# First expert weights loaded during routing, unused expert rows filled during the chunk scan, expert blocks run in pairs from block 0

## The reference, cut to what matters

```python
n_assign = n_tok * TOP_K
counts = jnp.bincount(flat_e, length=N_EXPERTS)
pcounts = (counts + (MOE_BLOCK - 1)) // MOE_BLOCK * MOE_BLOCK     # MOE_BLOCK = 128
pends = jnp.cumsum(pcounts); pstarts = pends - pcounts
dest = pstarts[se] + (arange(n_assign) - starts[se])
...
hdn = silu(xb @ w1[e]) * (xb @ w3[e])                            # w1, w3: 1024 x 512
return hdn @ w2[e]                                               # w2: 512 x 1024
...
y_assign = ybuf[dest] * sw[:, None]
y = segment_sum(y_assign, stok)
```

## Time and profile before

| | |
|---|---|
| time, median of 3 runs | 3274.21 us (3272.35 to 3277.04) |
| span of the profiled execution | 3280.3 us |
| the chunk scan's first load starts | 926.36 us |
| routing's last instruction starts (`idx`) | 2082.98 us |
| first expert matmul starts | 2101.44 us |
| last expert matmul starts | 3161.42 us |
| `combine` starts | 3165.65 us |
| PE busy, whole span | 2858.0 us (87%) |

### The profile page before, as it was taken

One profiled execution on the slowest core, in us unless ns is written; L12 is line 12 of the kernel. 1 busy time (PEld: TensorE's weight loads), 2 busy tenths in 40 slices (PEclk: granted clock), 3 DMA queues, 4 the chain that ended last, 5 costly groups with the idle time before them and its releaser, 6 DMA issues. The chain is left out here.

```text
span 3280.3 us, 48264 instructions
## 1 busy us (share of the span) xinstructions
PE 2858.0 (87%) x16338; PEld 2528.5 (77%) x16339; DVE 2044.5 (62%) x2266; ACT 974.9 (30%) x1814; POOL 1239.3 (38%) x929
## 2 busy tenths in 40 slices
PE   5999999999879999999997997497899999999940
PEld 4998989989758888888886886376777788778730
DVE  5464564645446766666673333879768567877836
ACT  5152341524422222222222221122223222223223
POOL 3010111001056666556662221443445445434434
PEclk6999999999989999999998998699999999999975
DMA  4011111111111110111104442489476566767649
GB/s 148 32 56 36 52 61 37 55 35 54 33 42 39 38 32 26 38 38 38 39 20 137 153 138 93 155 300 348 174 261 260 214 249 238 270 221 273 246 151 342
DMA packets 223030, 424.40 MB, mean 129 GB/s; under 512 B 14465, under 2 KB 103649, under 8 KB 222818
## 3 DMA queue, kind: packets, MB, share of 16 engines
q1 hardware_dynamic: 201984, 340.35, 29.7%
q0 software_dynamic: 13328, 55.06, 4.6%
q10 hardware_dynamic: 7634, 27.79, 2.1%
HBM read 343.31 MB, written 87.18 MB: 131 GB/s over the span
## 5 line engine op out<-in xcount | busy, mean ns | idle before, releaser
L450 PE MATMUL project_proj<-hT_high,project_w_high 128*128 128x412 f32 (+3 forms) x1392 | 496.5, 357 | 28.5 <-issue 10.9
L450 PE MATMUL project_proj<-hT_low,project_w_high 128*128 128x412 f32 (+3 forms) x1392 | 474.8, 341 | 0.0
L450 PE MATMUL project_proj<-hT_high,project_w_low 128*128 128x412 f32 (+3 forms) x1392 | 474.8, 341 | 0.0
L817 POOL TENSOR_TENSOR delta_M<-delta_lt,lvl 128x512 f32<-128x512 f32 x252 | 331.9, 1358 | 58.5 <-DVE delta_lt L1031 58.5
L1584 DVE TENSOR_TENSOR experts_w_low<-experts_w_whole,experts_w_high 128x2048 fp32r<-128x2048 f32 x128 | 349.3, 2729 | 4.4
L1678 PE MATMUL experts_h<-experts_w_high,experts_xT_high 128*128 x848 | 338.0, 399 | 12.0 <-POOL experts_xT_low L1628 7.8
L1678 PE MATMUL experts_h<-experts_w_low,experts_xT_high 128*128 x848 | 337.6, 398 | 0.0
L1678 PE MATMUL experts_h<-experts_w_high,experts_xT_low 128*128 x848 | 336.0, 396 | 0.0
L450 PEld LDWEIGHTS project_proj<-hT_high,project_w_high 128*128 128x128 f32 (+1 forms) x1392 | 261.3, 188 | 45.6 <-issue 31.9
L1582 DVE CAST experts_w_high<-experts_w_whole 128x2048 fp32r<-128x2048 f32 x128 | 190.8, 1491 | 169.2 <-DMA experts_w_whole<-in_w_dram 169.1
L866 PE MATMUL delta_prep<-delta_Tm,delta_M 128*128 128x128 f32 x1728 | 245.0, 288 | 49.8 <-DVE delta_qkT L1045 40.0
(11 more groups left out here) (270 smaller groups left out, 5727.5 us busy)
## 6 DMA issues: line engine op xcount, KB each, us to landing
experts_w_whole<-in_w_dram SPq DMA_DIRECT2D x128, 1024.0 KB, 10.5
experts_w_whole<-in_w_dram SPq DMA_DIRECT2D x32, 2048.0 KB, 18.4
delta_qkv<-feat SPq DMA_DIRECT2D x36, 768.0 KB, 4.7
y_rows<-experts_yout ACTq DMA_DIRECT2D x53, 512.0 KB
project_w_whole<-in_w_tiles_dram SPq DMA_DIRECT2D x28, 512.0 KB, 3.7
feat<-project_out SPq DMA_DIRECT2D x48, 205.0 KB, 1.9
normalise_x<-in_x_dram SPq DMA_DIRECT2D x18, 512.0 KB, 3.3
output_xres<-in_x_dram SPq DMA_DIRECT2D x18, 512.0 KB, 5.7
```

What stands on the lines that cost most here:

```text
L450: r = pe.matmul(dst, w[s][:, kt, 0:m], x[:, kt, lo:hi], start=kt == 0 and i == 0, stop=kt == KD - 1 and i == 2)
L817: pool.tensor_tensor(v["M"][:, l], v["lt"][:, :, :], bcast(k["lvl"][:, d, l, :], HEADS, 1), ALU.mult).then_inc(e["M_set"], 1)
```

## The change

Four things are done, all around the experts.

- `MAXB`, the largest number of blocks, is rounded to an even number (68, was 67), and the loop over pairs begins with the blocks 0 and 1. With 52 blocks, 52 run instead of 53. The last block to run, an odd number, comes from a new entry of `table`, which DVE writes at the end of routing.
- `empty_rows` is gone from POOL's loop. Instead SP fills, at the head of the chunk scan, all rows of `y_rows` from block `MINB` = 36 on: two DMAs of 2048 rows (8 MB each) from the input `x` to `y_rows`, ahead of the first load of the scan. Experts' blocks overwrite what is theirs later.
- A class `Weights` owns the weight buffers and is built ahead of `route`. SP loads w1, w3 and w2 of expert 0 and w1 and w3 of expert 1 while routing runs, and `experts` begins with expert 2 on SP. The wait for the first gather, which stood between two parts of expert 0's loads, goes with them.
- `ones`, `lower` and `lg` are placed at the other end of SBUF, and two index tiles become one; no instruction of theirs changes.

```diff
-MAXB += 1 - MAXB % 2
+MAXB += MAXB % 2
+MINB = 2 * T // P
...
+            rest = SLOTS - MINB * P
+            for half in range(2):
+                sp.dma_start(y_rows[MINB * P + half * rest // 2:MINB * P + (half + 1) * rest // 2, :], dram["x"][0:rest // 2, :]).then_inc(filled, 16)
             run(sp, step)
+            sp.wait_ge(filled, 32)
...
+        @block.sync
+        def _(sp):
+
+            weights.load_w13(sp, dram, 0, 0)
+            weights.load_w2(sp, dram, 0, 0)
+            weights.load_w13(sp, dram, 1, 1)
...
+            link(dve.tensor_scalar(tf[:, NE:NE + 1], end[:, NE - 1:NE], 1.0, None, ALU.subtract))
+            link(dve.tensor_copy(table[:, 2 * MAXB + NE + 1:2 * MAXB + NE + 2], tf[:, NE:NE + 1]))
+            link(dve.tensor_single_scalar(table[:, 2 * MAXB + NE + 1:2 * MAXB + NE + 2], table[:, 2 * MAXB + NE + 1:2 * MAXB + NE + 2], 1, ALU.bitwise_or))
             dve.wait_ge(placed, 1)
...
             step(0, 0, 0)
-            with eng.Fori(0, PAIRS) as j:
-                with eng.If(j * 2 + 1 < n):
+            step(1, 1, 0)
+            with eng.Fori(1, PAIRS) as j:
+                with eng.If(j * 2 < n):
+                    step(0, j * 2, j)
                     step(1, j * 2 + 1, j)
-                    step(0, j * 2 + 2, j + 1)
-                if and_then is not None:
-                    and_then(j)
+
+        def last_block(eng):
+            return eng.value_load(table[0:1, NB + 1:NB + 2], min_val=1, max_val=MAXB - 1)
...
-            load_w13(0, 0, PARTS[0:2])
-            sp.wait_ge(gathered, 16)
-            load_w13(0, 0, PARTS[2:])
-            load_w13(1, 1)
-            load_w2(0, 0)
...
-            def empty_rows(j):
...
-                with pool.If(j * -2 + (2 * PAIRS - 1) >= n):
-                    dst = y_rows[bass.ds(j * (-2 * P) + (2 * PAIRS - 1) * P, 2 * P), :]
-                    pool.dma_start(dst, xn_rows[0:2 * P, :]).then_inc(emptied, 16)
-                    pool.wait_ge(emptied, j * 16 + 16)
...
-            last = n // 2 * 2
+            last = last_block(pe)
             turn_gated(last)
             output(last)
```

More of the change, by code:

```diff
@@ L756, in delta @@
         E = [{n: b.sem(f"{n}{d}") for n in sems} for d in range(2)]
+        filled = b.sem("rows_filled")
         block = ctx.enter_context(nc.Block())
@@ L1317, in _, with __init__, load_w13, load_w2 @@
                     split(p, j * 2 + p)
-def route(nc, k, lg, gate, slot, table, idx):
+PARTS = [(n, q) for n in ("w1", "w3") for q in range(2)]
+KQ = KD // 2
+class Weights:
+    def __init__(self, nc, b):
+        whole, lows = over(nc, b, ("w1", "w3"), [P, 2, KD, FF])
+        self.whole, self.low = dict(zip(("w1", "w3"), whole)), dict(zip(("w1", "w3"), lows))
+        (self.w2_whole,), (self.w2_low,) = over(nc, b, ("w2",), [P, 2, FF // P, D])
+        self.w_sem = [{n: b.sem(f"moe_{n[0]}_{n[1]}_{p}") for n in PARTS} for p in range(2)]
+        self.w2_sem = [b.sem(f"moe_w2_{p}") for p in range(2)]
+    def load_w13(self, sp, dram, p, x):
+        for n, q in PARTS:
+            sp.dma_start(self.whole[n][:, p, q * KQ:(q + 1) * KQ],
+                         dram[n][bass.ds(x, 1), q * KQ * P:(q + 1) * KQ * P, :].rearrange("a (k p) n -> p (a k) n", p=P)).then_inc(self.w_sem[p][n, q], 16)
+    def load_w2(self, sp, dram, p, x):
+        sp.dma_start(self.w2_whole[:, p], dram["w2"][bass.ds(x, 1)].rearrange("a (k p) n -> p (a k) n", p=P)).then_inc(self.w2_sem[p], 16)
+def route(nc, k, dram, weights, lg, gate, slot, table, idx):
     with ExitStack() as ctx:
@@ L1484, in _, with experts @@
             dve.tensor_copy(idx[:, :], marked[:, :])
-def experts(nc, k, dram, table, idx, xn_rows, y_rows):
+def experts(nc, k, dram, weights, table, idx, xn_rows, y_rows):
     with ExitStack() as ctx:
@@ L1496, in experts @@
         pair = lambda name, shape, dt=F32: [b.sb(f"{name}{p}", shape, dt) for p in range(2)]
-        whole, lows = over(nc, b, ("w1", "w3"), [P, 2, KD, FF])
-        W = {n: (b.sb(f"{n}_high", [P, 2, KD, FF], F32R), low, w) for n, low, w in zip(("w1", "w3"), lows, whole)}
+        W = {n: (b.sb(f"{n}_high", [P, 2, KD, FF], F32R), weights.low[n], weights.whole[n]) for n in ("w1", "w3")}
         raw, xl = over(nc, b, ("xT0", "xT1"), [P, KD, P])
-        (w2_whole,), (w2_low,) = over(nc, b, ("w2",), [P, 2, FF // P, D])
+        w2_whole, w2_low = weights.w2_whole, weights.w2_low
         w2_high = b.sb("w2_high", [P, FF // P, D], F32R)
-        ix, xg = pair("ix", [P, 1], I32), b.sb("xg", [P, D])
+        both_ix, xg = b.sb("ix", [P, 2], I32), b.sb("xg", [P, D])
+        ix = [both_ix[:, p:p + 1] for p in range(2)]
         xh = pair("xT_high", [P, KD, P], F32R)
@@ L1573, in _ @@
             sp.wait_ge(e["done"], end_of(NE - 3))
-            load_w2(1, NE - 1)
+            weights.load_w2(sp, dram, 1, NE - 1)
         @block.vector
@@ L1660, in _ @@
             low(0, 0)
-            through_blocks(pool, n, step, empty_rows)
-            gated_low(n // 2 * 2)
+            through_blocks(pool, n, step)
+            gated_low(last_block(pool))
         @block.tensor
@@ L1780, in _ @@
             through_blocks(act, n, step)
[L1781 to L1785, removed]
+            last = last_block(act)
+            turned_gate(last)
+            act.wait_ge(e["gated_set"], last + 1)
+            output(last)
+            act.wait_ge(y_free, last * 16 + 32)
             act.sem_inc(e["all_stored"], 1)
@@ L1937, in encoder @@
                 with nc.cleanup_on_exit():
-                    delta(nc, k, gates, feat, O)
+                    delta(nc, k, dram, gates, feat, O, y_rows)
                 with nc.cleanup_on_exit():
                     output(nc, k, dram, feat, O, lg, x2_rows, xn_rows)
-        route(nc, k, lg, gate, slot, table, idx)
+        weights = Weights(nc, b)
+        route(nc, k, dram, weights, lg, gate, slot, table, idx)
         until_routed.close()
-        experts(nc, k, dram, table, idx, xn_rows, y_rows)
+        experts(nc, k, dram, weights, table, idx, xn_rows, y_rows)
         combine(nc, k, dram, gate, slot, x2_rows, y_rows, y)
```

35 lines of the change are left out of this document (12 added, 23 removed).

## The result

The changed kernel takes 3297.04 us (median of 4 runs, 3291.15 to 3297.58), the kernel before beside it 3275.62 (4 runs): a ratio of 1.0063, 95% interval [1.0049, 1.0078], or 21 us slower. The prediction was 3291.9 (3279 to 3310), slower.

The account below looks back on a forecast made before the run. Phases run in sequence; the scan is a PE-busy chain that cannot catch up, the experts PE-bound with a DVE-bound stretch. 44.6 - 9.2 - 17.7 = +17.7 us on a median of 3274.2 gives 3291.9 us, range 3279 to 3310.

Parts of the forecast that it names:

- Part 1: Head of the chunk scan: the first chunk lands only after the 16.78 MB fill, costing 44.6 us (38.4 to 60 likely).
- the fill does not hold up the scan: Rival, chance 0.11: chunk loads pass between the fill's pieces, as transfers on other queues do; about -23 us, 3251 us.
- the one queue: Argument against that rival: fill and chunk loads share SP's queue, which keeps its order.
- Part 2: Start of the experts: first weights loaded during routing gain 9.2 us (bounds 6 and 13), passed on by everything behind.
- the three terms: Block 0: first expert matmul 2.0 us sooner; w2 product's wait gone, 6.8 us; product 2.4 us shorter at the higher clock.
- Part 3: End of the experts: 52 blocks instead of 53 gain 17.7 us (bounds 15 and 18).
- Part 4: Experts' loop: no fills issued by POOL, taken as 0 since hidden in the DVE-bound stretch; 3 us allowed.

Follow-up runs that it names:

- fill_from_sbuf: Changed kernel with both fills read from a constant row in SBUF instead of DRAM, still on SP's queue ahead of the scan: 3286.24 us, 1.0030 of before.
- fill_on_act: Changed kernel with the same two fills issued at the same moment by ACT on its own queue instead of SP's: 3300.27 us, 1.0072 of before.
- fill_behind_first: Changed kernel with the two 8 MB fills issued one place later, behind the chunk loads of the scan's first step: 3260.85 us, 0.9955 of before.
- before_fill_head: Kernel before, with POOL's fills replaced by two fills ahead of the scan's first loads; late weights and 53 blocks kept: 3320.79 us, 1.0140 of before.
- before_fill_spread: Kernel before, with POOL's fills replaced by 16 pieces behind the scan's chunk loads; late weights and 53 blocks kept: 3270.64 us, 0.9987 of before.
- spread: Changed kernel with the fill cut into 16 pieces of 1 MB, one behind each scan step's chunk loads (steps 0 to 15): 3249.08 us, 0.9917 of before.
- spread_53: Changed kernel with the fill in 16 pieces in the scan and the earlier loop over pairs, so the empty block 52 runs: 3265.76 us, 0.9969 of before.

## Why the prediction was right, and where its terms were off

The forecast held: slower, by 21 us for 17.7 predicted, and for the reason given. By parts:

- **Part 1, +44.6 predicted, 50.6 in the trace** (47.8 and 50.2 by the runs). The mechanism was right on its place: the first chunk lands behind the fill, every engine waits, and the scan keeps its length. Mis-sized was the rate: 376 GB/s, from `combine` at its DMA share, against 332. The step that failed is "A fill reads and writes DRAM alike, so I take this". `combine` reads and writes DRAM too, but each of its bytes moves between DRAM and SBUF and touches DRAM once; in the changed kernel's trace it runs at 339 GB/s at a share of 0.90, as before. A copy's byte touches DRAM twice. `fill_from_sbuf`, with one touch, went at 404. The quiet 1 MB that seemed to go faster was a single copy, and said nothing on a long one. The Trainium skill's 716 GB/s for one core pair's memory (HBM Reference, Specifications (TRN2)), with both touches counted, gave an estimate of 46.9: nearer than my row, and still 3.7 us short, since 664 GB/s were reached.
- **Why it holds up the scan.** The rival "the fill does not hold up the scan" leaned on transfers on other queues that pass. For a fill in pieces of 64 KB that is wrong too: `fill_on_act` was no faster than the changed kernel. My argument against it, the one queue, is right for what is issued behind the fill (`fill_behind_first`), but is not the only thing that holds the chunk.
- **Part 2, -9.2 predicted, gains of 4.6 and 5.9 by two pairs of runs.** In the two profiles the three terms came as worked out: the first matmul 1.6 us sooner (2.0 predicted), the wait of 4.82 gone, the product 5.8 us in place of 8.2. At block 1 the changed kernel was 64.0 us behind routing's end where the kernel before was 72.7: 8.7. A third pair, the changed kernel against `before_fill_head`, gives 7.0 to 8.3: 25.3 for both parts, less 17.0 to 18.3 for part 3. The term took the wait of one execution as the rule. With late weights that wait was 4.82, 4.87 and 4.81, and in `before_fill_spread` 1.38 with no DVE behind it. Two of the estimates lie below my bound of 6 and one above, while each comes from ratios whose intervals reach 4 to 7 us to each side, and so they don't exclude 9.2. What the term is worth to better than that, and why one late execution did not wait, stays open.
- **Part 3, -17.7 predicted, gains of 17.0 and 18.3 by the runs.** Right. In the traces the stretch from the end of block 50's product to the start of the last one is 25.2 to 25.3 us in the four executions of 53 blocks and 8.3 in the nine of 52: 17.0. One step was off and cost little: PE's way out of the loop takes 3.23 us (3.21 in `spread`), where it took 1.31 before and takes 1.27 in `spread_53`, whose last block's number is worked out from a register. The load from `table` behind the loop was priced at 0.3; it takes 0.58 here, and 0.9 with what follows it. The rest is the loop itself, which the prediction left out: PE's sequencer, which issues its instructions, still goes through the pairs that don't exist, eight of them at 0.96 us each, where before it were seven at 0.74, and ends 2.1 us behind PE's last matmul and not 1.1. The wait for POOL behind it is 0.9 shorter in turn (4.39 against 5.25), so some 1.1 us are lost.
- **Part 4, 0 predicted, a gain of 4.3 by the runs**, interval 0 to 8.2, so my 3 is not excluded. Some of the 4.3 can be the clock: executions of either kernel have a mean granted clock near 0.93 or near 0.94, nine of the twelve of `before_fill_spread` the higher one and seven of the 17 of before beside them, and at the higher one the medians are 3270.24 and 3271.57. In the trace of before, blocks 12 to 14 take 38.4 us where the twelve executions without POOL's fills take 36.0 to 36.9; the last fill of the earlier trace rows is issued there, at 2415.2. The first and the last fill (2157.9 and 2415.2) lie outside the DVE-bound stretch of 2174 to 2345 us in which the prediction placed them all. That these 2 us come from the fills is argued from the place, in one execution of before, and not shown.

Parts 2 to 4 together were predicted at 26.9 and are 27.2 in `spread`. How parts 2 and 4 share it is known to a few us only, so that their sum came out so near is in part luck. The total is off by 3 us (20.6 against 17.7), about what part 1 is off by (47.8 against 44.6). The prediction's band of +8 to +36 is narrower than its own terms: a fill of 38.4 to 60 less gains of 34 to 21 gives +4 to +39. The measured 20.6 lies in both.

## What to carry to other kernels

A transfer that nobody waits for is free only if nothing urgent stands behind it or shares the DMA engines with it: put it behind the urgent loads, in pieces that fit the slack of one step, since here 16 pieces of 1 MB cost nothing and the same bytes in one go 48 us. Size a long copy by how often each byte touches DRAM, not by the busiest stretch of another kind, and price a wait that is to go away by more than one execution.

## What the runs showed of the hardware

- A copy of 16.8 MB within DRAM went at 332 GB/s, a fill of as much from SBUF at 404.
- Two queues with work went one piece against one, whatever the size (224 to 224 at 64 KB, 1354 to 1351 at 4 KB). So a transfer on another queue gave a chunk in 512 B pieces no way past while its own pieces were 64 KB, and let it through in some 20 us when they were 4 KB.
- Cutting the fill to 4 KB pieces did not slow it (51.8 against 50.6 us on SP's queue), but its issue held SP 10.9 us for the two where it took 1.28:

```profile
921.22 10.94 SPq L797 DMA_DIRECT2D y_rows<-in_x_dram  x2
...
978.13 0.71 PEld L878 LDWEIGHTS delta_prep<-ident,delta_qkv 128*128 128x128 f32 x4 [52.29 <-DMA delta_qkv<-feat]
```
